# Two chained transformer blocks on one core: the first tiles of h and their weight splits, side streams for rope angles and for scaling x, and the rope key's columns in a lora unit

## The reference, cut to what matters

```python
x = first_block(x, ...)        # h = rms_norm(x, norm1_w); h @ w_in; mixers; w_o; FFN; rms_norm(x, norm_f_w)
# second_block:
h = rms_norm_2(x, attn_norm_g)
proj = h @ w_in                              # r, k, v (3 x 1024), w 64, a 64, g 160, c_q 512, c_kv 512, k_pe 64
shifted = token_shift(proj[..., :3360], mu)  # of r, k, v, w, a, g alone
y_rwkv = rwkv7_mixer(r, k, v, w, a, g, ...)  # low-rank ("lora") maps of w, a, g; a recurrence over 256 tokens, 16 heads
q_pe = apply_rope_2(q[..., 128:], positions) # cos and sin of positions x inverse frequencies
k_pe = apply_rope_2(k_pe, positions)
y_mla = attention(rms_norm_2(c_q) @ w_uq, rms_norm_2(c_kv) @ w_ukv, q_pe, k_pe)
x = x + concat(y_rwkv, y_mla) @ w_out
x = x + conv_glu_ffn(rms_norm_2(x, ffn_norm_g), ...)
return rms_norm_2(x, final_norm_g)
```

## Time and profile before

| what | value |
|---|---|
| median of three runs | 2933.04 us (2932.98, 2933.04, 2936.99) |
| the profiled execution's own time | 2930.86 us |
| its span, first to last instruction | 2928.8 us |
| mean granted TensorE clock | 0.984 of full speed |
| TensorE matmul / weight load busy | 97% / 85% |
| VectorE, ScalarE, GpSimd busy | 70%, 47%, 16% |
| DMA | 475.73 MB, mean 162 GB/s |

### The profile page before, as it was taken

One profiled execution on the slowest core, in us unless ns is written; L12 is line 12 of the kernel. 1 busy time (PEld: TensorE's weight loads), 2 busy tenths in 40 slices (PEclk: granted clock), 3 DMA queues, 4 the chain that ended last, 5 costly groups with the idle time before them and its releaser, 6 DMA issues.

```text
span 2928.8 us, 41878 instructions
## 1 busy us (share of the span) xinstructions
PE 2837.5 (97%) x16472; PEld 2474.9 (85%) x16472; DVE 2054.2 (70%) x3131; ACT 1366.6 (47%) x2044; POOL 482.3 (16%) x530
## 2 busy tenths in 40 slices
PE   7999999999999999999999899999899999999997
PEld 6888888888888888888888788888788888888886
DVE  6886787766776666656667979756677777667655
ACT  5452454455554544444446444432454444434434
POOL 2120011110111111001002633610021111101102
PEclk9998999999999999999999999999999999999999
DMA  5443333445555555555556323311255555555554
GB/s 201 144 166 132 109 127 130 150 166 187 191 189 188 188 189 191 188 191 190 188 180 212 135 94 121 114 55 65 94 174 190 190 187 188 193 188 190 191 181 151
DMA packets 132242, 475.73 MB, mean 162 GB/s; under 512 B 14672, under 2 KB 14928, under 8 KB 131792
## 3 DMA queue, kind: packets, MB, share of 16 engines
q1 hardware_dynamic: 132048, 473.07, 48.6%
HBM read 470.92 MB, written 2.10 MB: 162 GB/s over the span
## 4 chain that ended last, share of the span: by engine, by line
PE 87%; DVE 10%; ACT 2%; issue 1%; DMA 0%; POOL 0%; DVEq 0%; ACTq 0%; SPq 0%; POOLq 0%
PE ps L864 86%; DVE U L1816 3%; DVE ringl L1816 2%; DVE U L1825 1%; ACT high L1372 1%; PE ps L867 1%; DVE U L1822 0%; DVE U L2022 0%; ACT U L1372 0%; DVE hr L1825 0%; DVE U L2013 0%; DVE hx L1816 0%; DVE xT L1816 0%; POOL U L2486 0%; DVE xT L1825 0%
## 5 line engine op out<-in xcount | busy, mean ns | idle before, releaser
L864 PE MATMUL ps<-hr,high 128*128 128x512 f32 x4688 | 1513.3, 401 | 25.5 <-DVE ringl L1816 18.6
L1816 DVE TENSOR_TENSOR ringl<-ring,high 128x1024 fp32r<-128x1024 f32 x882 | 1082.2, 1229 | 438.0 <-ACT high L1372 437.4
L1372 ACT ACTIVATE high<-ring 128x1024 fp32r<-128x1024 f32 x882 | 916.3, 1041 | 651.4 <-PE ps L864 635.7
L864 PEld LDWEIGHTS ps<-hr,ringl 128*128 128x128 f32 x4688 | 883.7, 189 | 208.0 <-issue 2.2
L864 PE MATMUL ps<-hr,ringl 128*128 128x256 f32 x4688 | 924.3, 279 | 0.0
L864 PEld LDWEIGHTS ps<-hr,high 128*128 128x128 f32 x4688 | 724.7, 189 | 32.3 <-issue 21.6
L864 PE MATMUL ps<-yur,high 128*128 128x512 f32 x2176 | 685.3, 396 | 12.6 <-DVE yur L1816 12.4
L2486 POOL TENSOR_TENSOR U<-U,rs 128x256 f32<-128x256 f32 x293 | 266.4, 909 | 1746.1 <-DVE U L1816 1714.3
L1372 ACT ACTIVATE U<-ps 128x256 f32<-128x256 f32 (+5 forms) x482 | 173.4, 371 | 684.1 <-PE ps L864 664.8
L864 PEld LDWEIGHTS ps<-yur,ringl 128*128 128x128 f32 x2176 | 412.1, 189 | 92.8 <-issue 0.2
L864 PE MATMUL ps<-yur,ringl 128*128 128x256 f32 x2176 | 432.4, 280 | 0.0
(11 more groups left out here) (168 smaller groups left out, 1255.7 us busy)
## 6 DMA issues: line engine op xcount, KB each, us to landing
ring<-in_w_dram SPq DMA_DIRECT2D x872, 512.0 KB, 3.7
ring<-in_w_dram SPq DMA_DIRECT2D x32, 256.0 KB, 3.3
xT<-in_x_dram SPq DMA_DIRECT2D x4, 512.0 KB, 6.7
out_dram<-hx SPq DMA_DIRECT2D x4, 512.0 KB, 3.0
cst<-in_cst_dram SPq DMA_DIRECT2D x1, 1438.5 KB, 12.7
yT<-in_lora_dram SPq DMA_DIRECT2D x1, 1024.0 KB, 6.8
U<-in_lora_dram SPq DMA_DIRECT2D x1, 512.0 KB, 4.8
posi<-in_pos_dram SPq DMA_DIRECT2D x1, 128.0 KB, 3.9
```

The lines of the kernel that those rows point to most:

```text
L864: return e.matmul(out, l, r, start=start, stop=stop)
L1372: return e.activation(out, i, ACT.Copy, scale=scale)
L1816: return e.tensor_tensor(out, a, b, op)
```

## The change

Four edits:

1. Start: SyncE's order becomes a quarter of x, a block, four times over. ScalarE and VectorE split block i right after the quarter i of h (i below 3); all squares come after all of `hh`. ScalarE first makes a copy of one column that needs the first constants alone.
2. The angles leave the lora stream for one of their own, `trig`, in five steps, not before the first unit of the third pair of heads (`rw`, 2, 0) is there. Scratch is now two tiles of `ckvT`, so ScalarE's evacuation of `lat` unit 4 waits for the cosine's angle. The recurrence starts after two lora steps in place of three.
3. Scaling x becomes a side stream `xs` of eight steps of two tiles, not before the last `rw` unit. Evacuations of the first `wout` units wait for it; `mla` takes `yT`'s tile 4 as scratch in place of `rtmp`.
4. The 64 columns of the rope key go into the zeros of the third lora unit; the `kpe` unit (blocks 560, 561) is gone, and two copies of 64 partitions on VectorE, in `lora1`, put the key in place.

```diff
-    for j, cl in enumerate((C128(RK0), C128(RK0 + 128), list(range(RK0 + 256, RK0 + 288)) + [-1] * 96)):
+    last = list(range(RK0 + 256, RK0 + 288)) + [-1] * 32 + list(range(CQ0 + 1024, CQ0 + 1088))
+    for j, cl in enumerate((C128(RK0), C128(RK0 + 128), last)):
         p.cols("lora", (j,), "w_in_2", 16, cl)
...
-            pe_cols = list(range(CQ0 + 1024, CQ0 + 1088))
-            p.cols("kpe", (), "w_in_2", 16, pe_cols + pe_cols)
...
-        sides["lora"] = [("lora0", [("DVE", 5.8), ("ACT", 2.2)], [("used", mark["main2"] + 3)]),
-                         ("lora1", [("DVE", 2.6), ("ACT", 2.4)], need(("lora", 2))), ("lora2", [("DVE", 1.0)], [])]
+        sides["lora"] = [("lora1", [("DVE", 3.2), ("ACT", 2.4)], need(("lora", 2))), ("lora2", [("DVE", 1.0)], [])]
+        sides["trig"] = [("cast", [("DVE", 2.5)], need(("rw", 2, 0))), ("sin0", [("DVE", 1.5)], []), ("sin1", [("DVE", 1.5), ("ACT", 1.8)], []),
+                         ("cos0", [("DVE", 1.1)], []), ("cos1", [("DVE", 1.9), ("ACT", 1.8)], [])]
+        sides["xs"] = [("xs", [("DVE", 0.95)], need(("rw", 7, 2))) for _ in range(8)]
-            of = {"lw": [("lora", 3)], "fin": [("mla", 4)]}
+            of = {"lw": [("lora", 2)], "fin": [("mla", 4)]}
...
-                elif u.kind == "lat" and key[0] == 0:
-                    e.wait_ge(ldve.sem, ldve.after("pos"))
+                elif u.kind == "lat" and key[0] in (0, 4):
+                    e.wait_ge(ldve.sem, ldve.after("pos" if key[0] == 0 else "cos"))
...
 ScalarE, main:
+                copy(sg[1][:, 0:1], C("eps")).then_inc(mact.sem, mact.inc())
                 for i in range(4):
                     e.wait_ge(s_x[i], 16)
                     for t in range(4 * i, 4 * i + 4):
                         copy(hh[:, t, :], xT[:, t, :], scale=C("norm1", t, t + 1)).then_inc(mact.sem, mact.inc("hh", "norm1", t))
-                    if i == 0:
-                        split(0)
-                    for j in (2 * i, 2 * i + 1):
...
-                for m in range(1, AHEAD):
-                    split(m)
+                    if i < AHEAD:
+                        split(i)
+                for j in range(8):
+                    if j >= 2:
+                        e.wait_ge(mpool.sem, mpool.after("acc", "norm1", 2 * max(1, j - 2) + 2))
+                    e.activation(sqs[:, j % 2, :], xT_[:, 512 * j:512 * j + 512], ACT.Square)\
+                        .then_inc(mact.sem, mact.inc("sq", "norm1", 2 * j + 1))
...
 VectorE, main:
                 for t in range(16):
                     low_of("norm1", t)
-                    if t == 3:
-                        split(0)
-                for m in range(1, AHEAD):
-                    split(m)
+                    if t % 4 == 3 and t // 4 < AHEAD:
+                        split(t // 4)
...
-                    if mark["main2"] + 4 <= m < mark["main2"] + 12:
-                        for t in range(2 * (m - mark["main2"] - 4), 2 * (m - mark["main2"] - 4) + 2):
-                            stt(xT[:, t, :], xT[:, t, :], C("normf", t, t + 1), rtmp, MUL, MUL).then_inc(mdve.sem, mdve.inc())
...
 VectorE, in the lora stream:
+                for a in (0, 64):
+                    e.tensor_copy(kpe[a:a + 64, 0, :], lraw[64:128, 2, 1:257]).then_inc(ldve.sem, ldve.inc("kpe") if a else ldve.inc())
...
 SyncE:
             for i in range(4):
                 c = slice(4 * SEQ * i, 4 * SEQ * (i + 1))
                 e.dma_start(xT_[:, c], d_x[:, c]).then_inc(s_x[i], 16)
-                if i == 0:
-                    load(0)
-            for m in range(1, 4):
-                load(m)
+                load(i)
```

More of the change, by code:

```diff
@@ L844, in normed @@
         def normed(u):
-            return u.kind in ("gates", "dn", "q", "kc", "vc", "ks", "kw", "mg", "gate", "fup", "lora", "rw", "lat", "kpe")
+            return u.kind in ("gates", "dn", "q", "kc", "vc", "ks", "kw", "mg", "gate", "fup", "lora", "rw", "lat")
         rs_read = {"norm2": index[("mg", 1, 15)], "attn_g": index[("fup", 1, 43)], "ffn_g": index[("rw", 7, 2)],
@@ L1321, in mla_first @@
                     yield f"rq{a}"
-                e.wait_ge(mpool.sem, mpool.after("sc", index[("kpe",)]))
+                e.wait_ge(ldve.sem, ldve.after("kpe"))
                 rope(kpe[:, 0:1, :], 2, 1)
@@ L1700, in lora, with trig @@
                 yield "lora1"
+            def trig():
+                e.wait_ge(ldve.sem, ldve.after("sin"))
+                e.activation(sin2, sin2, ACT.Sin).then_inc(lact.sem, lact.inc("sin"))
+                yield "sin1"
+                e.wait_ge(ldve.sem, ldve.after("cos"))
+                e.activation(cos2, cos2, ACT.Sin).then_inc(lact.sem, lact.inc("cos"))
+                yield "cos1"
             def rwkv(s):
@@ L1809, in _ @@
                 ("gates", gates()), ("dn", deltanet()), ("nsa", nsa_first()), ("nsa0", nsa(0)), ("nsa1", nsa(1)),
[L1810 removed]
+                ("lora", lora()), ("trig", trig()), ("rw0", rwkv(0)), ("rw1", rwkv(1)), ("mla", mla_first()), ("mla0", mla(0)), ("mla1", mla(1)))])
         @block.vector
@@ L1873, in evac0 @@
                     e.wait_ge(used.sem, used.after(u.end()))
+                    if u.kind == "wout" and key[0] == 0:
+                        e.wait_ge(ldve.sem, ldve.after("xs", key[1]))
                     for j in range(2):
@@ L2269, in nsa, with scaled, trig @@
                     yield "sm2"
-            def lora():
-                n, a = lh[:, 0, :], lh[:, 1, :]
+            def scaled():
+                for t in range(16):
+                    stt(xT[:, t, :], xT[:, t, :], C("normf", t, t + 1), rtmp, MUL, MUL).then_inc(ldve.sem, ldve.inc("xs", t))
+                    if t % 2:
+                        yield "xs"
+            def trig():
+                n, a = ckvT[:, 0, :], ckvT[:, 1, :]
                 e.wait_ge(s_pos, 16)
                 e.tensor_copy(a, posi[:, :]).then_inc(ldve.sem, ldve.inc("pos"))
+                yield "cast"
+                e.wait_ge(ldve.sem, ldve.after("pos"))
+                ts1(a, a, C("inv2"), MUL).then_inc(ldve.sem, ldve.inc("angle"))
                 e.wait_ge(ldve.sem, ldve.last())
[L2276 to L2279, removed]
+                for name, dst, shift_ in (("sin", sin2, 0.0), ("cos", cos2, float(np.float32(np.pi / 2)))):
+                    ts(n, a, 1.0 / (2 * np.pi), shift_ / (2 * np.pi), MUL, ADD).then_inc(ldve.sem, ldve.inc())
                     e.wait_ge(ldve.sem, ldve.last())
@@ L2282, in lora @@
                     e.wait_ge(ldve.sem, ldve.last())
-                    ts1(n, n, 12582912.0, SUB).then_inc(ldve.sem, ldve.inc())
-                    e.wait_ge(ldve.sem, ldve.last())
+                    ts1(n, n, 12582912.0, SUB).then_inc(ldve.sem, ldve.inc("turns", name))
+                    yield name + "0"
+                    e.wait_ge(ldve.sem, ldve.after("turns", name))
                     stt(dst, n, -6.28125, a, MUL, ADD).then_inc(ldve.sem, ldve.inc())
@@ L2291, in lora @@
                     e.wait_ge(ldve.sem, ldve.last())
-                    if shift:
-                        ts1(dst, dst, shift, ADD).then_inc(ldve.sem, ldve.inc())
+                    if shift_:
+                        ts1(dst, dst, shift_, ADD).then_inc(ldve.sem, ldve.inc())
                         e.wait_ge(ldve.sem, ldve.last())
                     ts(dst, dst, 3.1415925, -3.1415925, ALU.min, MAX).then_inc(ldve.sem, ldve.inc(name))
-                    e.wait_ge(ldve.sem, ldve.last())
-                yield "lora0"
+                    yield name + "1"
+            def lora():
                 e.wait_ge(mpool.sem, mpool.after("sc", index[("lora", 2)]))
@@ L2428, in mla_first @@
                         e.wait_ge(ape.sem, ape.after("ss", 0))
+                        e.wait_ge(adve.sem, adve.after("n", 0))
                     tt(yT[:, 4:8, :], src, src, MUL).then_inc(adve.sem, adve.inc("sq", c))
@@ L2725 @@
         dst = w[at:at + 128 * kt * n].reshape(128, kt, n)
-        real = [c for c in cl if c >= 0]
-        if real == list(range(real[0], real[0] + len(real))):
-            part = src[:, real[0]:real[0] + len(real)]
-        else:
-            part = src[:, real]
-        dst[:, :, len(real):] = 0
-        dst[:, :, :len(real)] = part.reshape(kt, 128, len(real)).transpose(1, 0, 2)
+        if cl == list(range(cl[0], cl[0] + n)):
+            part = src[:, cl[0]:cl[0] + n]
+        else:
+            part = np.where(np.array(cl) >= 0, src[:, cl], 0)
+        dst[:] = part.reshape(kt, 128, n).transpose(1, 0, 2)
         at += 128 * kt * n
```

24 lines of the change are left out of this document (6 added, 18 removed).

## The result

The changed kernel takes 2944.67 us (median of six runs, 2943.49 to 2946.49) against 2933.22 (2931.04 to 2936.99): 1.0038 times as long, 95% interval 1.0025 to 1.0051. That is 11.5 us slower, where 13 us less were forecast, and outside the range of 2910 to 2930. Rival E (2935 up) had the sign.

The account below looks back on a forecast made before the run. TensorE's matmuls, covering 97% of the span, were taken to bound the kernel. 3.0 + 10.9 + 4.5 - 4 - 1.5 = 12.9, taken as 13 us with order effects not worked out: 2920 us, range 2910 to 2930.

Parts of the forecast that it names:

- Rival E: Moved VectorE work delays the recurrence's chain by every microsecond, and new waits bring cold spells: 2935 up, to 2941; 5%.
- Start, +3.0: Kernel start: earlier copy and interleaved loads gain 2.8 to 3.3 us, 3.0 taken, carried along behind the sums.
- The burst, +10.9: Head of main2 without the angle burst: waits of 6.63 and 2.52 us and a 1.7 us cold spell go; bounds 8.4 and 10.9.
- both waits: TensorE in main2's head: 6.63 us at the third lora unit, 2.52 us at the recurrence's first matmuls; both forecast to go.
- kpe, +4.5: Main blocks: eight matmul pairs less take 5.7 us off TensorE; bounds 0 and 5.7, 4.5 taken.
- The angles' new place, -4: Near 1653 us, 8.5 us of VectorE work arrives where VectorE is 95% busy; bounds 0 and 8.5, 4 lost.
- rival C: VectorE's full stretch from 1650 us takes the angles in full, 8.5 us: gain 8.4, time 2925; 18%.
- Scaling x, -1.5: Near 1900 us, 7.6 us of VectorE work returns in eight steps, two in the way; bounds 0 and 7.6, 1.5 lost.
- the stretch after 1900 has over 30 us of idle time: TensorE after 1900 us, idle 21 us before; over 30 us would show the prediction wrong.
- The cast: Cast of the positions, first of the moved angle work, expected near 1650 us as a sign of the forecast.
- wait from 1650 to 1725 us: TensorE where VectorE is nearly full: new waits over 3 us would show the prediction wrong.
- From the recurrence's first matmuls to its end about as long as before: Length of the recurrence, expected about unchanged as a sign that the forecast holds.

Follow-up runs that it names:

- e8: Whole change, but the stage's steps stand where the kernel before had them, angle and scaling steps early: 2927.18 us, ratio 0.9983 to the kernel before.
- e5: Kernel before, order kept, 14 of the 17 VectorE angle instructions left out of the burst: 2929.06 us for 2932.39, ratio 0.9982.
- e6: e2's kernel in its own new order, with the angle work cut as in e5: 2942.90 us, ratio 1.0044 to the kernel before.
- e7: e2's instructions, other steps placed as in the kernel before, angle steps between blocks 524 and 533: 2928.91 us for 2932.39, ratio 0.9991.
- e11: e8 with angle steps (blocks 535 to 547) and scaling (584.5 to 587.5) placed as in the changed kernel: 2927.20 us for 2932.80, ratio 0.9977.
- e1: Kernel before with the start's edit alone: 2932.52 us for 2933.79, ratio 1.0000.
- e3: Kernel before with the rope key's columns in the lora unit, alone, steps placed by the planner: 2932.39 us, ratio 0.9990.
- e2: Kernel before with the angle stream moved, alone, steps placed by the planner: 2945.51 us, ratio 1.0036.
- e4: Kernel before with the scaling of x moved behind the last r, k, v unit, alone, steps placed by the planner: 2941.38 us, ratio 1.0023.
- e12b: Whole change, steps placed as in the earliest-ending of 24 planner draws with 1% cost noise, angles and scaling early: 2920.83 us for 2933.52, ratio 0.9957.

## Why the prediction was wrong

**The step that failed** is in the sum: "with the fixed order shaken up by an amount I can't work out: 13 us". An amount that could not be worked out went in as zero, and in no range. It is the largest term of all: 16.7 us between e8 (-5.2) and the changed kernel (+11.5), 13.8 between e5 and e6, and -9.6 to +21.1 with nothing else changed. The price per part was read from the rows of before as if the list stayed; only e5, e7, e8 and e11 have such a list. What the new list does is use the weight blocks up early: the recurrence's last pairs then run without any beside them, for 101.9 us in place of 34.7.

The terms, each with what was measured:
- **Start, +3.0.** Shape right (blocks 1 and 2 by 21 us, a gap of 6.67 where 5.6 was worked out, a cold block 3, sums at 32.4 and not 31). e1: 0.0. "Behind the sums nothing changes, so the gain is carried along" is wrong: the clock fell a second time and took most of the 1.6 us that were left (e1's trace shows the same, pairs 1.28 us apart from 40.27). The prediction priced a fall only behind waits of more than 2.8 us; this one came behind a wait of 1.69.
- **The burst, +10.9.** In the changed kernel both waits vanish as said. In before's order the first does, but the second grows (4.20 us in e5, 2.82 in e7, 3.59 in e8) and brings a spell at the lower clock, which takes 1.6 to 3.0 us. e5 is worth 3.3 us (2.6 to 7.6), below the lower bound of 8.4. The head's gain is real (a lead of 8.5 us in e7 and e8), but isn't carried to the end.
- **kpe, +4.5.** e3: 1.4 (0.3 to 5.6), within the bounds, in a list of its own that the planner rates 3.8 units worse. In before's order e8's trace gains 3.7 us between the second and the third square root: about right.
- **The angles' new place, -4.** By whole times 0: e7 against e5 0.2 us less, e11 against e8 none, each with an interval of some 5 us. By the lead it was about right or too small: some 4.3 us in e7 and e8, 7.3 in e11, where the steps stand later and rival C's 8.5 is nearer. Burst and angles together, forecast +6.9, are 3.5 (e7). As the planner places them, -11.7 (e2).
- **Scaling x, -1.5.** e11 against e8: 0 at the late places. As the planner places it, -7.6 (e4).

In before's order the five come to 5.2 us (e8), where 12.9 were worked out; that error alone would have left the time inside the range, at 2928. E had the right side for the wrong cause: its mechanism, moved work that delays the recurrence by its own time to the end, is refuted by e6 and e11. Its second half, waits that bring the low clock, is what the end of the changed kernel shows.

**The signs named beforehand.** "Wrong if the stretch after 1900 has over 30 us of idle time": it came true. Until 2078 us TensorE is idle for 21.2 us, as before, but the stretch now ends with the out product at 2095.89, and up to there it is 31.4; its clock is 0.86 for 0.95. The cast came at 1663.95 us, not near 1650. No wait from 1650 to 1725 us is over 3 us (the longest is 1.93). "From the recurrence's first matmuls to its end about as long as before" failed too: 435 us became 467 (to the last square root).

**What stays open.** Which of the many moved steps makes a list bad, and so empties its end of weight blocks, wasn't tried one by one. Why a lead of 8.7 us at e11's third square root is 3.8 at the eighth isn't known either. How much of the 15 us is the low clock and how much the chain with nothing beside it is an estimate (5.8 us for the eighty matmuls), with no run that parts them. Why the out product's first wait is 7.5 us in one list, 5.1 in another and none in e12b was not tested by itself.

## What to carry to other kernels

Where a greedy planner writes the order, every edit of a step or a cost is two changes: the work, and a new draw of the list. Freeze the list to price the work; draw many lists with noise on the costs to see how far the list alone moves the time, and take a good one. And price a wait that goes away by what lies behind it, not by its own length: here a new wait with its spell at the lower clock, and the same work at its new place on a full VectorE, took back 6 to 8 of the 8.5 us. Then look whether the last stretch still has work of another stream to run beside its chain.

## What the runs showed of the hardware

- TensorE busy 24.48 of 25 us (2050 to 2075 us) and still at a granted clock of 0.50, 1.2 GHz, the work there being single matmuls of 128x64 and 128x128; 3.63 us of idle time came just before. In the recurrence's earlier stretches, where the same forms stand between blocks of 128x512, the clock is 1.00. The Trainium skill, TensorE: Matmul & The Clock Gate, "What's actually happening", says that activity releases the throttle; in these 25 us the trace doesn't agree, as TensorE counts as busy for 98% of them and keeps the lower clock.
- The clock fell within about 1 us of the end of a wait of 1.69 us at 37.56 us in the changed kernel, and stayed up behind a wait of the same length at 39.19 us in before.
- The clock of one and the same stretch (250 to 310 us) varies between executions from 0.69 to 0.80, and moves all behind it by up to 5 us. Spans should be compared from a mark behind such a stretch.
- The cast of the positions took 2.39 us at the head of main2, and 0.26 us at 1663.95 us in the changed kernel, for the same 128x256 elements. In before and in e5 the slow cast overlaps six GpSimd memsets in a row and ends 0.15 us after the last of them; the fast one starts in the gap between two GpSimd instructions. That the cast waits for GpSimd is likely by this, and wasn't tested.
- A table load of ScalarE takes 1.28 us and no more: 36 of the 58 in before have less than 0.1 us of idle time in front and behind together.
